# The rings of weight slabs move from the start of the SBUF partition to its end

## The chip, the cores and the metric

The kernel runs on one core of one Trainium2 chip. The metric is the device time of one execution in microseconds (us), as the median of several runs. Engines are named as the profile names them: PE is TensorE's matmuls and PEld its weight loads, DVE is VectorE, ACT is ScalarE, POOL is GpSimd, SP is the engine that issues nearly all DMA transfers.

## What is computed

Two blocks, one after the other, on 256 tokens of width 1,024, all in float32. The reference, cut to its frame:

```python
def first_block(x, ...):                      # DEPTH = 2 layers
    for l in range(DEPTH):
        h = rms_norm(x, norm_mix[l])
        proj = h @ w_in[l]                    # 1024 x 5120
        y_a = dilated_attention(dq, dk, dv) @ w_proj_a[l]
        y_b = stick_breaking_attention(sq, sk, sv) @ w_proj_b[l]
        gates = jax.nn.sigmoid(gate_logits + b_gate[l])
        x = x + (gates[..., :D_MODEL] * y_a + gates[..., D_MODEL:] * y_b) @ w_out[l]
        x = x + conv_ffn(rms_norm(x, norm_ffn[l]), w_up[l], conv_w[l], conv_b[l], w_down[l])
    return rms_norm(x, norm_final)

def hybrid_layer(x, ...):                     # second block, one layer
    proj = rmsnorm(x, norm_mix_w) @ w_in      # conv, gated delta rule, gated linear recurrence
    x = x + concat(gdn_out, lru_out) @ w_out
    u = relu(rmsnorm(x, norm_mlp_w) @ w_ff1)
    x = x + (u * u) @ w_ff2
```

## The kernel before

**Slabs.** Every large weight matrix is cut into slabs of at most 128 partitions by 2,048 float32 values (`SLAB`), mostly 256 output columns of the matrix in 8 chunks of 128 rows. `Plan` lists them once, in the order in which TensorE consumes them. A slab goes through three steps:

1. SP loads it from HBM into the ring `raw` (L648).
2. ACT writes its high part, rounded to the format `float32r`, into the ring `w_hi` (its copies all pass through one helper, so they show as L1329).
3. DVE (L1861) or, for a few slabs, POOL (L2614) writes the low part, `raw` minus `w_hi`, into the ring `w_lo`.

**Rings.** Each of the three rings has `SLOTS` = 3 slots of 2,048 values, that is 24,576 bytes in each partition. Slab n uses slot n modulo 3 of all three. SP loads slab n when the low part of slab n - 3 is written, since then nothing reads that slot of `raw` any more. ACT overwrites a slot of `w_hi` when the matmuls of slab n - 3 are done.

**Matmuls.** TensorE multiplies each chunk of a slab three times: high weight by high activation, high weight by low activation, low weight by high activation. The helper on L679 issues them. In most tiles the weights are the stationary operand and the activations (`xg_hi`, `xg_lo`, or the pairs in `hid_both`) the moving one of 256 columns; where a high part meets a `hid_both` pair, the high and low activations go through together as 512 columns. Only in the slabs of values and in the very last product are the weights the moving operand. The first slab alone is multiplied straight from `raw` in float32, by activations in `scratch`.

**The other tensors.** `xt` is the running x, `consts` and `params` are tables, `sq`, `rs`, `cs`, `rtok`, `gfg2` and `small` are small working tensors, and `scratch` (14,976 values) holds everything else: the token input, queries and keys, gates, attention probabilities `prob` and their transposes, the convolution rows, the output rows. Attention turns `prob` blocks on TensorE with the identity from `consts` (L906), and the last stage turns `xt` in the same way (L1259).

**Who is ordered by what.** Each engine's program is written out by hand in its order, with semaphores between engines. No order and no wait depends on where a tensor lies in the partition.

**Where a tensor lies.** The function `sb` asks for the tensors one after another, and the allocator puts each behind the one before, from byte 16,512 of the partition on (16,384 bytes and four small constants of the framework lie below), each start rounded up to a multiple of 32 bytes. The three rings are the first three requests; `scratch` is the last, and it ends at byte 225,632.

Of the kernel before, what the change touches and what calls it, by code (L numbers as in the profile page):

```python
# [25 lines left out]
F32R = mybir.dt.float32r  # L26
# [63 lines left out]
SLOTS = 3  # L90
RAWS = 1
IDLE_TURNS = 12
SLAB = 2048
# [305 lines left out]
def build(nc, w, consts_d, params_d, lru_d, out):  # L399
    plan = Plan(w)  # L400
    with ExitStack() as ctx:
        S = {n: ctx.enter_context(nc.semaphore(n)) for n in SEMS}

        def sb(name, cols, dt=F32):
            return ctx.enter_context(nc.sbuf_tensor("sb_" + name, [P, cols], dt))[:, :]

        raw = sb("raw", SLOTS * SLAB)
        w_hi = sb("w_hi", SLOTS * SLAB, F32R)
        w_lo = sb("w_lo", SLOTS * SLAB, F32R)
        xt = sb("xt", KD * T)  # L410
        xg_hi = sb("xg_hi", KD * T, F32R)
        xg_lo = sb("xg_lo", KD * T, F32R)
# [7 lines left out]
        gfg2 = sb("gfg2", KD)  # L420
        small = sb("small", 144)
        scratch = sb("scratch", SCRATCH)
        psum = ctx.enter_context(nc.psum_tensor("psum", [P, 8, 512], F32))

        def C(name, a=0, b=None):
# [2287 lines left out]
```

How the kernel before makes its waits and increments, by code:

```python
        @block.sync  # L623
# [13 lines left out]
                load_x(n)  # L637
            s = plan.slabs[0]
            for name, chunks in (("load_half", slice(0, KD // 2)), ("slab_in0", slice(KD // 2, KD))):
                eng.dma_start(by_chunk(raw, s)[:, chunks, :], s.src.rearrange("(k p) c -> p k c", p=P)[:, chunks, :])\
                    .then_inc(S[name], 16)
            for s in plan.slabs[1:]:
                if s.n >= SLOTS:
                    name, value = plan.slabs[s.n - SLOTS].low
                    if q.due(name, value):
                        eng.wait_ge(S[name], value)
                eng.dma_start(by_chunk(raw, s), s.src.rearrange("(k p) c -> p k c", p=P))\
                    .then_inc(S[f"slab_in{s.n % SLOTS}"], 16)
                if s.n == 2:
                    eng.dma_start(COS.bitcast(I32), w["positions"].to_broadcast([P, T])).then_inc(S["load_pos"], 16)
                    eng.dma_start(cst[:, EARLY:], consts_d[:, EARLY:]).then_inc(S["load_rest"], 16)
                if s.stage == (2, "in") and s.index == 3:
                    if q.due("q_tile", 12 * DEPTH):
                        eng.wait_ge(S["q_tile"], 12 * DEPTH)
                    eng.dma_start(l_w, lru_d).then_inc(S["load_lru"], 16)
                if s.stage == (2, "up", 0) and s.index == 3:
                    if q.due("x_tile", KD + 24 * DEPTH + 2 * KD):
                        eng.wait_ge(S["x_tile"], KD + 24 * DEPTH + 2 * KD)
                    if q.due("hid_lo", LO_BEFORE_MLP):
```

## Time and profile before

| | |
|---|---|
| median of 3 runs | 1070.47 us (1070.12 to 1070.49) |
| span of the profiled execution | 1068.9 us |
| PE busy | 1054.3 us (99%) |
| PEld busy | 1003.1 us (94%) |
| DVE busy | 720.5 us (67%) |
| ACT busy | 573.1 us (54%) |
| POOL busy | 284.9 us (27%) |
| mean DMA rate | 169 GB/s |

The span runs from the first to the last instruction of one profiled execution; the timed runs lie 1.6 us above it. Busy time of PE counts pipelined matmuls from issue to modelled end, so that two neighbours overlap: the pace of a stretch is read from the starts of its matmuls, and what sets the end of the program from the chain of work that ended last. A granted clock of 1.00 is TensorE at 2.4 GHz, 0.50 at 1.2 GHz.

### The profile page before, as it was taken

The numbers are of one execution on the slowest core, as the hardware profiler recorded it, in microseconds if no ns is written. First come the engines' busy times: TensorE is split into PE (matmuls) and PEld (weight loads), VectorE is DVE, ScalarE is ACT, GpSimd is POOL, SyncE is SP. The second block draws the span as 40 slices with busy tenths as digits, with TensorE's granted clock in tenths as the row PEclk, the third lists the DMA queues.
The fourth block names the chain that finished last, engine by engine and source line by source line (L and its number), as shares of the span: only waits on it lengthen the run. The fifth ranks groups of instructions, "written<-read, shape, count | busy, mean of one in ns | idle before, by whom it ended". The sixth has DMA issues, their size and how long they took to land.

```text
span 1068.9 us, 20016 instructions
## 1 busy us (share of the span) xinstructions
PE 1054.3 (99%) x8398; PEld 1003.1 (94%) x8398; DVE 720.5 (67%) x1217; ACT 573.1 (54%) x791; POOL 284.9 (27%) x179
## 2 busy tenths in 40 slices
PE   8999999999999999999999999999899999999997
PEld 7999998999999899999999989998899999999996
DVE  5762248887677775322878857777887789666763
ACT  6454466654354644545765534556557865343443
POOL 0376665100000137666640000013300034101020
PEclk9999999999999999999999999999999999999999
DMA  9644444465653664444456566446333157563751
GB/s 308 202 161 140 156 159 158 163 212 157 222 193 124 214 215 158 131 148 150 157 165 213 160 217 200 132 147 217 110 94 116 60 178 224 186 209 126 249 170 40
DMA packets 169705, 180.11 MB, mean 169 GB/s; under 512 B 4240, under 2 KB 166416, under 8 KB 169488
## 3 DMA queue, kind: packets, MB, share of 16 engines
q1 hardware_dynamic: 169616, 178.84, 52.3%
q8 instruction: 66, 1.08, 0.4%
q14 instruction: 23, 0.19, 0.1%
HBM read 177.78 MB, written 1.05 MB: 167 GB/s over the span
## 4 chain that ended last, share of the span: by engine, by line
PE 88%; DVE 4%; ACT 3%; POOL 2%; issue 1%; DMA 1%; SPq 0%; POOLq 0%; ACTq 0%; DVEq 0%
PE psum L679 87%; DVE sb_w_lo L1861 2%; POOL sb_w_lo L2614 1%; ACT sb_scratch L1329 1%; ACT sb_w_hi L1329 1%; DVE sb_xg_lo L1845 1%; POOL sb_scratch L2654 1%; DMA sb_raw<-in_w_in 1%; PE psum L906 1%; DVE psum L1845 1%; DVE sb_scratch L1845 0%; ACT L1329 0%; DVE sb_hid_both L1936 0%; DVE sb_xt L1879 0%; DVE sb_scratch L2439 0%
## 5 line engine op out<-in xcount | busy, mean ns | idle before, releaser
L1329 ACT ACTIVATE sb_w_hi<-sb_raw 128x2048 fp32r<-128x2048 f32 (+3 forms) x185 | 318.2, 1724 | 175.4 <-PE psum L679 111.1
L679 PE MATMUL psum<-sb_xg_hi,sb_w_hi 128*128 128x256 f32 x1656 | 411.9, 287 | 0.0
L679 PE MATMUL psum<-sb_xg_lo,sb_w_hi 128*128 128x256 f32 x1656 | 406.6, 284 | 0.0
L1861 DVE TENSOR_TENSOR sb_w_lo<-sb_raw,sb_w_hi 128x2048 fp32r<-128x2048 f32 (+3 forms) x150 | 305.6, 2040 | 110.7 <-ACT sb_w_hi L1329 109.9
L679 PEld LDWEIGHTS psum<-sb_xg_hi,sb_w_hi 128*128 128x128 f32 x1656 | 317.3, 192 | 3.2 <-DVE sb_xg_lo L1845 0.7
L679 PEld LDWEIGHTS psum<-sb_xg_lo,sb_w_hi 128*128 128x128 f32 x1656 | 317.9, 192 | 0.3
L679 PE MATMUL psum<-sb_xg_hi,sb_w_lo 128*128 128x256 f32 x1656 | 233.7, 284 | 0.1
L679 PEld LDWEIGHTS psum<-sb_xg_hi,sb_w_lo 128*128 128x128 f32 x1656 | 213.6, 192 | 0.9 <-DVE sb_w_lo L1861 0.3
L679 PE MATMUL psum<-sb_hid_both,sb_w_hi 128*128 128x512 f32 (+1 forms) x912 | 210.0, 364 | 0.4 <-DVE sb_xt L1879 0.2
L2614 POOL TENSOR_TENSOR sb_w_lo<-sb_raw,sb_w_hi 128x2048 fp32r<-128x2048 f32 (+1 forms) x34 | 156.1, 4598 | 110.3 <-ACT sb_w_hi L1329 100.8
L679 PEld LDWEIGHTS psum<-sb_hid_both,sb_w_hi 128*128 128x128 f32 x912 | 150.4, 190 | 20.8 <-issue 0.8
L679 PEld LDWEIGHTS psum<-sb_hid_both,sb_w_lo 128*128 128x128 f32 x784 | 112.5, 190 | 9.4
L679 PE MATMUL psum<-sb_hid_both,sb_w_lo 128*128 128x256 f32 x784 | 119.7, 283 | 0.0
L2630 POOL TENSOR_TENSOR sb_rs<-sb_sq 128x256 f32<-128x256 f32 x6 | 4.8, 804 | 325.4 <-ACT sb_sq L1329 325.4
L1329 ACT ACTIVATE sb_hid_both<-sb_scratch 128x256 fp32r<-128x256 f32 x100 | 38.5, 414 | 98.3 <-DVE sb_scratch L2151 68.8
L2686 POOL TENSOR_TENSOR sb_scratch<-sb_scratch 128x256 f32<-128x256 f32 x32 | 23.3, 751 | 123.2 <-DVE sb_scratch L1845 123.2
L1329 ACT ACTIVATE sb_scratch<-sb_scratch,sb_params 128x256 f32<-128x256 f32 x76 | 37.8, 554 | 31.3 <-DVE sb_scratch L2148 31.3
L1936 DVE TENSOR_TENSOR sb_hid_both<-sb_scratch,sb_hid_both 128x256 fp32r<-128x256 f32 x100 | 50.7, 545 | 4.8 <-ACT sb_hid_both L1329 4.3
L679 PE MATMUL psum<-sb_scratch 64*64 64x32 f32 (+6 forms) x728 | 49.7, 263 | 3.0 <-ACT sb_scratch L1329 3.0
L2020 DVE CUSTOM_DVE_ANT_0 sb_scratch<-psum,sb_consts 128x512 f32<-128x512 f32 x16 | 10.4, 689 | 61.9 <-PE psum L679 61.9
L679 PEld LDWEIGHTS psum<-sb_scratch 64*64 64x64 f32 (+3 forms) x728 | 42.0, 152 | 8.9 <-ACT sb_scratch L1329 3.2
L1329 ACT ACTIVATE sb_scratch<-psum 128x256 f32<-128x256 f32 (+3 forms) x58 | 24.6, 463 | 47.7 <-PE psum L679 28.6
(172 smaller groups left out, 986.1 us busy)
## 6 DMA issues: line engine op xcount, KB each, us to landing
sb_raw<-in_w_in SPq DMA_DIRECT2D x51, 1024.0 KB, 5.2
sb_raw<-in_w_up SPq DMA_DIRECT2D x44, 1024.0 KB, 5.1
sb_raw<-in_w_ff SPq DMA_DIRECT2D x21, 1024.0 KB, 5.7
sb_raw<-in_w_down SPq DMA_DIRECT2D x16, 768.0 KB, 4.7
sb_raw<-in_w_down SPq DMA_DIRECT2D x16, 640.0 KB, 4.4
sb_raw<-in_w_out SPq DMA_DIRECT2D x8, 1024.0 KB, 5.1
sb_raw<-in_w_ff SPq DMA_DIRECT2D x8, 768.0 KB, 4.6
sb_raw<-in_w_ff SPq DMA_DIRECT2D x8, 640.0 KB, 4.5
```

The lines of the kernel that those rows point to most:

```text
L679: return nc.tensor.matmul(ps, lhsT, rhs, start=start, stop=stop, skip_group_check=True)
L906: mm = nc.tensor.transpose(psum[:, BANK_T + u % 2, i * P:i * P + P], prob_of(u)[:, i * P:i * P + P], C("ident"))
L1329: return nc.scalar.activation(out_, in_, func, **kw)
L1845: return v.scalar_tensor_tensor(out=out_, in0=a, scalar=scalar, in1=b, op0=op0, op1=op1)
L1861: v.tensor_tensor(part(w_lo, s), part(raw, s), part(w_hi, s).bitcast(F32), ALU.subtract)\
L1936: v.tensor_tensor(hid_lo(i), src, hid_hi(i).bitcast(F32), ALU.subtract).then_inc(S["hid_lo"], 1)
L2020: v.tensor_tensor_reduce(prob_of(u), psum[:, BANK_SC + u % 2, :], C(f"dil_mask{units(u)[1]}"), -HEAD ** -0.5, 3e38, ALU.add, ALU.min, dil_ ...
L2614: g.tensor_tensor(part(w_lo, s), part(raw, s), part(w_hi, s).bitcast(F32), ALU.subtract)\
L2630: g.tensor_tensor(SUMS[n], tl(sq, 2 * n) if m == 1 else SUMS[n], tl(sq, 2 * n + m % 2), ALU.add)\
L2654: g.tensor_tensor(tl(mix32, m % 4), tl(mixA, m % 2), tl(mixB, m % 4), ALU.add)\
L2686: g.tensor_tensor(tl(h32, i % 4), tl(y_conv, i % 4), tl(y_conv, i % 4), ALU.mult)\
```

## The change

The three lines that allocate `raw`, `w_hi` and `w_lo` move from the head of the list of tensors to its end, behind `scratch`. Nothing else differs.

```diff
-        raw = sb("raw", SLOTS * SLAB)
-        w_hi = sb("w_hi", SLOTS * SLAB, F32R)
-        w_lo = sb("w_lo", SLOTS * SLAB, F32R)
         xt = sb("xt", KD * T)
         xg_hi = sb("xg_hi", KD * T, F32R)
...
         small = sb("small", 144)
         scratch = sb("scratch", SCRATCH)
+        raw = sb("raw", SLOTS * SLAB)
+        w_hi = sb("w_hi", SLOTS * SLAB, F32R)
+        w_lo = sb("w_lo", SLOTS * SLAB, F32R)
         psum = ctx.enter_context(nc.psum_tensor("psum", [P, 8, 512], F32))
```

The order of instructions on PE, DVE, ACT, POOL and SP is the same in both programs, row for row, with the same operands, shapes and waits. What differs is the start address, in bytes from the start of each partition:

| tensor | bytes | start before | start after | remainder by 64, before and after |
|---|---|---|---|---|
| `raw` | 24,576 | 16,512 | 151,904 | 0, 32 |
| `w_hi` | 24,576 | 41,088 | 176,480 | 0, 32 |
| `w_lo` | 24,576 | 65,664 | 201,056 | 0, 32 |
| `xt` | 8,192 | 90,240 | 16,512 | 0, 0 |
| `xg_hi` | 8,192 | 98,432 | 24,704 | 0, 0 |
| `xg_lo` | 8,192 | 106,624 | 32,896 | 0, 0 |
| `hid_both` | 24,576 | 114,816 | 41,088 | 0, 0 |
| `consts` | 9,920 | 139,392 | 65,664 | 0, 0 |
| `cs` | 4,096 | 160,992 | 87,264 | 32, 32 |
| `scratch` | 59,904 | 165,728 | 92,000 | 32, 32 |

Every tensor that isn't a ring comes down by 73,728 bytes, which is 36 times 2,048. The rings go up by 135,392 bytes, which is 66 times 2,048 and 224 over; their distances from each other stay. Before, `prob`, part of `scratch`, starts at byte 206,688; after, `w_lo` covers bytes 201,056 to 225,632.

## Rows read from the trace of the kernel before

**Rows 1.** The chain that ended last: shares by line, and its first piece (start, us)
```profile
PE psum L679 87%; DVE sb_w_lo L1861 2%; POOL sb_w_lo L2614 1%; ACT sb_scratch L1329 1%; ACT sb_w_hi L1329 1%; DVE sb_xg_lo L1845 1%; POOL sb_scratch L2654 1%; DMA sb_raw<-in_w_in 1%; PE psum L906 1%; DVE psum L1845 1%; DVE sb_scratch L1845 0%; ACT L1329 0%; DVE sb_hid_both L1936 0%; DVE sb_xt L1879 0%; DVE sb_scratch L2439 0%
...
3.63 6.53 DMA sb_raw<-in_w_in
```

**Rows 2.** Two stretches: length, busy us of PE, PEld, DVE, ACT, POOL, clock, DMA share, GB/s
```profile
142.00:175.00 33.00, 32.84 (x240) 30.49 (x239) 22.79 (x40) 22.91 (x39) 23.14 (x14) 1.00 0.51 162
...
733.00:854.00 121.00, 117.57 (x1314) 110.46 (x1311) 95.44 (x209) 81.69 (x143) 18.25 (x8) 0.99 0.35 109
```

**Rows 3.** Costliest groups of the page: moving then stationary operand, xcount | busy, mean ns
```profile
L679 PE MATMUL psum<-sb_xg_hi,sb_w_hi 128*128 128x256 f32 x1656 | 411.9, 287 | 0.0
L679 PE MATMUL psum<-sb_xg_lo,sb_w_hi 128*128 128x256 f32 x1656 | 406.6, 284 | 0.0
...
L679 PE MATMUL psum<-sb_xg_hi,sb_w_lo 128*128 128x256 f32 x1656 | 233.7, 284 | 0.1
...
L679 PE MATMUL psum<-sb_hid_both,sb_w_hi 128*128 128x512 f32 (+1 forms) x912 | 210.0, 364 | 0.4 <-DVE sb_xt L1879 0.2
...
L679 PE MATMUL psum<-sb_hid_both,sb_w_lo 128*128 128x256 f32 x784 | 119.7, 283 | 0.0
```

**Rows 4.** Timeline of PE at 95 us: start, us, instruction
```profile
95.43 0.28 PE L679 MATMUL psum<-sb_xg_lo,sb_w_hi 128*128 128x256 f32 x1
95.55 1.12 PE L679 MATMUL psum<-sb_xg_hi,sb_w_lo 128*128 128x256 f32 x8
```

**Rows 5.** Instructions of L906, L1259, sb_raw, sb_cs: xcount: ns min/median/max, first and last start
```profile
L906 PE MATMUL psum<-sb_consts,sb_scratch x64: 270/273/273, 96.5 to 501.6; 128*128 128x128 f32 x64
...
L906 PEld LDWEIGHTS psum<-sb_consts,sb_scratch x64: 138/141/144, 96.4 to 501.5; 128*128 128x128 f32 x64
...
L1259 PEld LDWEIGHTS psum<-sb_consts,sb_xt x16: 139/140/143, 1019.3 to 1021.0; 128*128 128x128 f32 x16
L1259 PE MATMUL psum<-sb_consts,sb_xt x16: 271/273/273, 1019.5 to 1021.1; 128*128 128x128 f32 x16
...
L679 PEld LDWEIGHTS psum<-sb_scratch,sb_raw x32: 187/190/191, 10.2 to 16.8; 128*128 128x128 f32 x32
...
L679 PEld LDWEIGHTS psum<-sb_scratch,sb_cs x16: 187/191/192, 803.0 to 821.7; 128*128 128x128 f32 x16
```

**Rows 6.** Groups of DVE, ACT and POOL, shapes kept apart, 1,024 values per partition
```profile
L1861 DVE TENSOR_TENSOR sb_w_lo<-sb_raw,sb_w_hi 128x1024 fp32r<-128x1024 f32 x6 | 7.3, 1218 | 1.7 <-ACT sb_w_hi L1329 1.7
...
L2417 DVE TENSOR_TENSOR sb_scratch<-sb_scratch 128x1024 f32<-128x1024 f32 x1 | 1.2, 1226 | 0.0
L1329 ACT ACTIVATE sb_w_hi<-sb_raw 128x1024 fp32r<-128x1024 f32 x8 | 8.3, 1048 | 2.5 <-PE psum L679 2.5
...
L1329 ACT ACTIVATE sb_scratch<-sb_scratch 128x1024 f32<-128x1024 f32 x3 | 3.2, 1055 | 0.5 <-DVE sb_scratch L2417 0.5
L2614 POOL TENSOR_TENSOR sb_w_lo<-sb_raw,sb_w_hi 128x1024 fp32r<-128x1024 f32 x2 | 4.7, 2392 | 32.2 <-ACT sb_w_hi L1329 32.2
...
L2677 POOL TENSOR_TENSOR sb_sq<-sb_sq,sb_scratch 128x1024 f32<-128x1024 f32 x1 | 2.4, 2362 | 51.1 <-ACT sb_sq L1329 51.1
```

**Rows 7.** DMA: hardware queue of the page, SP's longest wait, two windows (last two: share, GB/s)
```profile
q1 hardware_dynamic: 169616, 178.84, 52.3%
...
SPq L648 <- DVE sb_w_lo L1861: 731.0, 147, 14.5
...
12.00:13.00 1.00, 1.00 (x6) 0.87 (x6) 1.00 (x4) 1.00 (x5) 0.00 (x0) 1.00 1.11 349
...
889.00:890.00 1.00, 1.00 (x11) 1.00 (x10) 1.00 (x1) 0.00 (x0) 1.00 (x1) 1.00 1.04 366
```

**Rows 8.** Three windows around 760 us, columns as in rows 2 (the clock is third from last)
```profile
758.00:760.00 2.00, 0.57 (x5) 0.57 (x6) 1.31 (x4) 1.28 (x3) 0.00 (x0) 1.00 1.01 352
760.00:762.00 2.00, 2.00 (x15) 2.00 (x14) 0.93 (x8) 2.00 (x3) 0.00 (x0) 0.65 0.41 137
762.00:764.00 2.00, 2.00 (x11) 2.00 (x10) 1.65 (x12) 1.95 (x2) 0.00 (x0) 0.50 0.00 0
```

## The prediction

> **What bounds the kernel now.** I read the chain of work that ended last first, because it says which engine's time is the program's time: the helper through which TensorE's matmuls are issued holds 87% of it [rows 1]. The rest, some 13% or 139 us of the profiled 1068.9 us, is spread over DVE, ACT, POOL and DMA. Then come the stretches: in the two where TensorE hands over most often, its busy time is still 32.84 of 33.00 us and 117.57 of 121.00 us [rows 2]. So the kernel goes at the pace of its matmuls. Third, the costliest groups: 1656 + 1656 + 1656 + 912 + 784 = 6,664 matmuls take their stationary operand from `w_hi` or `w_lo`, which are two of the three tensors that change their place [rows 3]. Fourth, their pace from the timeline: one starts at 95.43 us and the next at 95.55, 0.12 us later, and the eight behind it fill 1.12 us, which is seven steps of 0.12 us and one duration of 0.28 [rows 4]. The question of this case is therefore narrow: does TensorE's 0.12 us step, or any duration beside it, depend on the address of an operand?
>
> **The change, part by part.** No instruction is added, removed or reordered, no wait and no semaphore differs, and no transfer changes its size, so there is no queue past which anything moves. What can change is the duration of work that touches a moved address. Three properties of an address differ: the rings' remainder by 64 bytes (0 before, 32 after), their position (all three then lie where `scratch` lay before, `w_lo` under its tail), and their distance to the activations. The other tensors keep their remainder by 2,048 and only come down; I cost them at nothing, since their neighbours in the rows below show no dependence on position either.
>
> (a) Weight loads and matmuls. The trace has the same operation on both kinds of address. The transposes of L906 take `prob` as their stationary operand, at byte 206,688 and above with a remainder of 32 by 64: just the kind of address the rings get. Those of L1259 take `xt`, at byte 90,240, remainder 0: the kind that the rings leave. Their weight loads have a median of 141 and 140 ns, their matmuls of 273 and 273 ns [rows 5]. A second pair is of the weight loads ahead of float32 matmuls of 256 columns: 190 ns with `raw` as stationary operand (remainder 0), 191 ns with `cs` (remainder 32) [rows 5]. The two ends for a ring matmul are thus 0 and +1 ns. For 6,664 of them +1 ns would be 6.7 us. I take 0, because the PE matmul of the closest pair, L906 against L1259, does not differ at all and the weight load, which differs by 1 ns in the median, lies beside the matmul before it, and because ranges within each group (138 to 144, 139 to 143) are wider than the difference. Below nothing: a stationary load of ring data would have to gain from the new place; neither pair shows the higher or odd address as the cheaper one. Term: 0 us.
>
> Distance to the activations: before, a matmul of `xg_hi` with `w_hi` joins tensors 57,344 bytes apart, and one with `w_lo` 32,768 bytes apart. Both step by 0.12 us [rows 4], 287 and 284 ns mean [rows 3]. A pace that hung on the distance would show two values here. Term: 0 us.
>
> (b) Splits. The copies into `w_hi` and the subtractions into `w_lo` touch only ring tensors, whose distances stay. With 1,024 values per partition, DVE takes 1218 ns on ring addresses and 1226 on `scratch` (remainder 32); ACT 1048 against 1055; POOL 2392 against 2362 [rows 6]. So the bounds are +0.7% for DVE and ACT, and -1.3% for POOL. On the chain they have 2% (DVE L1861), 1% (ACT) and 1% (POOL L2614) [rows 1], some 21, 11 and 11 us. The term lies between 21 x 0.7% + 11 x 0.7% = +0.2 us and 11 x -1.3% = -0.1 us. The rows compare an operation of one kind with one of another, so this small difference need not be of the address; I take 0.
>
> (c) Transfers into `raw`. They keep their size and number and arrive at a start with remainder 32. The hardware queue is busy for 52.3% of the span, and SP stands 731.0 us in 147 waits for a slot that DVE frees [rows 7]: a somewhat longer transfer is taken from that wait, and ends at no engine. Only the first load is exposed, 6.53 us of the chain [rows 1]. A comparison: between 12 and 13 us, with slabs going to ring addresses, the DMA moves 349 GB/s at a share of 1.11, that is 314 per full share; between 889 and 890 us, when the output gain is being spread into `scratch` (remainder 32) beside slabs, 366 at 1.04, that is 352 [rows 7]. The second has larger pieces, so it is no clean measure, but it excludes that a start with remainder 32 is costly. Bounds: 314 / 352 is -11% of 6.53 us, -0.7 us; the mirror of it above is +0.7 us. I take 0.
>
> The rows point to no dependence at all. The Trainium skill has one rule that would: "DMA: Bandwidth & Descriptors", section "How a descriptor splits into AXI transactions", says that a transfer not starting at a multiple of 256 bytes first goes down to the boundary below and pays for the bytes in between. It speaks of what is fetched; if it held for the SBUF side of these loads too, a piece of 1,024 bytes would be an estimated 36 beats before (remainder 128 by 256) and 35 after (remainder 96), the exposed load would be 3% or 0.2 us shorter, and the sum -0.2 us in place of 0. No row here shows single beats.
>
> (d) The clock. At 760 to 764 us the granted clock is 0.65 and then 0.50, behind a window in which TensorE was busy for only 0.57 of 2 us; the lost time is 2 x 0.35 + 2 x 0.50 = 1.7 us [rows 8]. It is at the level of 1.2 GHz for that stretch. If a small shift in time let it come otherwise, the sum could move by 1.7 us either way, still under 0.2%. I take 0.
>
> Sum: 0 us against the profiled span of 1068.9 us, which with the 1.6 us outside the span gives the median as it was: 1070.5 us.
>
> **The rivals.** About 0.2%, 2.1 us, is what a measurement of this kernel can tell from no change.
>
> Slower, by the matmuls: operands with a remainder of 32 by 64, or at the end of the partition, cost TensorE's read a step. For it speaks only that weight loads of `cs` and `prob` have a median 1 ns above their partners; against it that the matmuls of L906 and L1259 are equal [rows 5]. At +1 ns for each of 6,664 matmuls the time is 1070.5 + 6.7 = 1077.2 us; if only the 1656 + 784 = 2,440 with `w_lo` pay, 1072.9 us. It decides from 2.1 us / 6,664 = 0.3 ns each. Chance 5%.
>
> Slower, by the transfers: writes to the new addresses take longer by a factor f. The first load alone makes 0.2% at f = 1.33 (6.53 x 0.33 = 2.1 us). Later it decides where DMA becomes the bound, at f = 1 / 0.523 = 1.9; with f = 2 the queue would be busy 1068.9 x 0.523 x 2 = 1118 us, and the time about 1120 us. Against it is the window at 889 us [rows 7]. Chance 2%.
>
> Faster: the old neighbourhood of rings and activations costs TensorE something that the new one doesn't. No row names what makes up the step of 0.12 us, so it could hold such a cost; against it is that the step is the same for both distances [rows 4]. 1 ns less each gives 1070.5 - 6.7 = 1063.8 us. Chance 3%.
>
> The change does not do what it says: the allocator could sort its requests, and the addresses would stay. It doesn't, since the built program has the new starts; and the time would be 1070.5 us all the same. Inside the forecast.
>
> Clock and chance: two or more stretches at the lower clock come or go, at 1.7 us each, 1067 or 1074 us. 1% each way.
>
> **How the numbers follow.** The forecast, no change, has 88%. Faster by over 0.2% is 3% + 1% = 4%; slower is 5% + 2% + 1% = 8%; within 0.2% is 88%. The range takes in the bounds that were left open: splits -0.1 and +0.2, the first load -0.7 and +0.7, the clock -1.7 and +1.7, together -2.5 and +2.6 us, so 1068.0 to 1073.1 us. That also holds the rival in which only `w_lo` pays, and leaves out under 1 in 10.
>
> **What would show it.** Right: the slab matmuls still step by 0.12 us with means of 284 and 287 ns, LDWEIGHTS of the rings have the same mean, the 2,048-value splits of the three engines keep theirs, the first DMA piece of the chain is near 6.5 us, and the chain is at TensorE's helper for 87%. Wrong: a step of 0.121 us or more (or below 0.119), or ring weight loads longer than those of other operands, tells of TensorE; longer splits in the two stretches of handovers, without a change in the step, tell of the engines; more "DMA" among the releasers of ACT's copies tells of the transfers. What would make the prediction wrong as a whole is a property of the partition that no tensor of the kernel before exposes, such as one that shows only when the moving operand, the stationary operand and a write are all at particular places at once.

## The result and the profile after

The changed kernel takes 1056.22 us (median of 4 runs, 1055.63 to 1059.37), the kernel before 1070.48 us beside it: a ratio of 0.986, 95% interval 0.9844 to 0.9877. The forecast was no change, 1070.5 us, range 1068.0 to 1073.1. It was wrong: a change of addresses alone gained 1.4%. The profiled execution has a span of 1053.9 us, 15.0 us under the one before.

The page after, from its groups (operands as in [rows 3]; xcount | busy, mean ns | idle before):

```profile
L679 PE MATMUL psum<-sb_xg_hi,sb_w_hi 128*128 128x256 f32 x1656 | 401.8, 283 | 0.1
L679 PE MATMUL psum<-sb_xg_lo,sb_w_hi 128*128 128x256 f32 x1656 | 396.7, 279 | 0.0
...
L679 PE MATMUL psum<-sb_xg_hi,sb_w_lo 128*128 128x256 f32 x1656 | 228.3, 280 | 0.1
L679 PE MATMUL psum<-sb_hid_both,sb_w_hi 128*128 128x512 f32 (+1 forms) x912 | 210.5, 364 | 1.3 <-DVE sb_xt L1874 0.6
...
L679 PE MATMUL psum<-sb_hid_both,sb_w_lo 128*128 128x256 f32 x784 | 118.2, 279 | 0.0
```

Against [rows 3], every group of 256 columns is 3 to 5 ns shorter (287 to 283, 284 to 279, 284 to 280, 283 to 279), and the group that is mostly of 512 columns is not (364 and 364). The timeline of PE shows the pace (start, us, instruction):

```profile
93.24 0.28 PE L679 MATMUL psum<-sb_xg_lo,sb_w_hi 128*128 128x256 f32 x1
93.35 0.28 PE L679 MATMUL psum<-sb_xg_hi,sb_w_hi 128*128 128x256 f32 x1
93.47 0.28 PE L679 MATMUL psum<-sb_xg_lo,sb_w_hi 128*128 128x256 f32 x1
93.59 0.28 PE L679 MATMUL psum<-sb_xg_hi,sb_w_hi 128*128 128x256 f32 x1
93.70 0.28 PE L679 MATMUL psum<-sb_xg_lo,sb_w_hi 128*128 128x256 f32 x1
...
94.52 1.10 PE L679 MATMUL psum<-sb_xg_hi,sb_w_lo 128*128 128x256 f32 x8
```

Four steps take 93.70 - 93.24 = 0.46 us, where each took 0.12 before [rows 4]. A finer measure is used from here on: in a stage of even tiles, the starts of two neighbouring groups of eight matmuls with `w_lo` are one tile of 24 matmuls apart. Starts are shown to 0.01 us, so such a step is good to 0.4 ns. The first two lines are of the kernel before, the last two of the one after:

```profile
208.08 1.12 PE L679 MATMUL psum<-sb_xg_hi,sb_w_lo 128*128 128x256 f32 x8
210.96 1.12 PE L679 MATMUL psum<-sb_xg_hi,sb_w_lo 128*128 128x256 f32 x8
```

```profile
208.26 1.10 PE L679 MATMUL psum<-sb_xg_hi,sb_w_lo 128*128 128x256 f32 x8
211.06 1.10 PE L679 MATMUL psum<-sb_xg_hi,sb_w_lo 128*128 128x256 f32 x8
```

2.88 us / 24 = 120.0 ns before, 2.80 us / 24 = 116.7 ns after. That is under the 0.119 us which the prediction named as the sign that TensorE's work had changed. The weight loads of the rings that stand beside these matmuls are shorter too, with a mean of 188 ns against 192. The other engines' work is nearly what it was: DVE is busy for 720.2 us (720.5 before), ACT 572.9 (573.1), POOL 287.1 (284.9), and the hardware DMA queue for 53.0% of the span against [rows 7]'s 52.3%.

**Where the 15 us come from.** I summed the distances between the starts of all matmuls of both traces. 5,899 steps of the slab matmuls of 256 columns with a stationary ring operand (gaps above 130 ns left out) take 706.5 us before and 689.3 after: -17.2. Gaps behind slab matmuls grow from 31.2 to 33.6 us: +2.4. The last stage, 512 columns with the ring as the moving operand, goes from 27.0 to 27.8 us: +0.8. The rest is -1.0, and it is the clock's: before, the granted clock is 0.50 for 3.4 us from 760.6 us on [rows 8], and in the profile after there is no such drop at that place. TensorE starts 26 matmuls between 760 and 764 us before, and 40 in the four microseconds after that do the same work (749 to 753, clock 1.00). Step by step, the matmuls under the drop are 1.6 us slower than the same ones after: 1.0 us of it in the rest, 0.6 in the gaps. So some 1.6 of the 15.0 us are not the step's, but an event that differs from one execution to the next; the kernel `a2_front_shifted` below has the same step, keeps the drop (at 749.5 us), and has a span of 1054.9 us. The grown gaps stand where TensorE now reaches the other engines. The chain, cut to the end of the second half of `w_down` in layer 0, before and then after (shares by line of that stretch):

```profile
by line: PE psum L679 100.7%
...
343.83 30.22 PE psum L679 x179
```

```profile
by line: PE psum L679 31.4%; DVE sb_w_lo L1861 24.2%; ACT sb_w_hi L1329 15.2%; DVE sb_xt L1879 9.1%; DVE sb_xt L1877 7.3%; ACT sb_xg_hi L1329 5.3%; issue 4.5%; DVE sb_xg_lo L1845 4.2%; ACT sb_sq L1329 0.3%; ACTq L1342 0.1%
...
348.67 1.29 ACT sb_w_hi L1329
349.98 1.49 DVE sb_w_lo L1861
```

Before, that stretch was TensorE's alone. With a shorter step, much of what ends last in it is work of DVE and ACT, the splits of the slabs above all.

### The profile page after: what moved, and what is told of

Same layout as the page of the kernel before. It is cut to its first block, busy times and chain, and to the rows that moved or that the text cites. A ratio compares the mean times of both kernels' runs of the same rounds, so it can differ in the third digit from the quotient of the medians.

```text
span 1053.9 us, 20016 instructions
## 1 busy us (share of the span) xinstructions
PE 1039.0 (99%) x8398; PEld 984.3 (93%) x8398; DVE 720.2 (68%) x1217; ACT 572.9 (54%) x791; POOL 287.1 (27%) x179
## 4 chain that ended last, share of the span: by engine, by line
PE 84%; DVE 7%; ACT 4%; POOL 2%; issue 2%; DMA 1%; SPq 0%; POOLq 0%; ACTq 0%; DVEq 0%
PE psum L679 83%; DVE sb_w_lo L1861 2%; POOL sb_w_lo L2614 1%; ACT sb_scratch L1329 1%; ACT sb_w_hi L1329 1%; DVE sb_xg_lo L1845 1%; DVE psum L1845 1%; POOL sb_scratch L2654 1%; DMA sb_raw<-in_w_ff 1%; DMA sb_raw<-in_w_in 1%; PE psum L906 1%; DVE sb_hid_both L1936 0%; DVE sb_xt L1879 0%; DVE sb_scratch L1845 0%; DVE sb_xt L1877 0%
## 5 line engine op out<-in xcount | busy, mean ns | idle before, releaser
L679 PE MATMUL psum<-sb_xg_hi,sb_w_hi 128*128 128x256 f32 x1656 | 401.8, 283 | 0.1
L679 PE MATMUL psum<-sb_xg_lo,sb_w_hi 128*128 128x256 f32 x1656 | 396.7, 279 | 0.0
L679 PEld LDWEIGHTS psum<-sb_xg_hi,sb_w_hi 128*128 128x128 f32 x1656 | 310.3, 187 | 3.3 <-DVE sb_xg_lo L1845 0.8
L679 PEld LDWEIGHTS psum<-sb_xg_lo,sb_w_hi 128*128 128x128 f32 x1656 | 310.7, 188 | 0.3
L679 PE MATMUL psum<-sb_xg_hi,sb_w_lo 128*128 128x256 f32 x1656 | 228.3, 280 | 0.1
L679 PEld LDWEIGHTS psum<-sb_xg_hi,sb_w_lo 128*128 128x128 f32 x1656 | 207.9, 187 | 1.0 <-DVE sb_w_lo L1861 0.3
```

What stands on the lines that cost most here:

```text
L679: return nc.tensor.matmul(ps, lhsT, rhs, start=start, stop=stop, skip_group_check=True)
```

## Experiments

Three theories stood against each other. **C**: the step depends on where a matmul's stationary operand lies relative to its moving one. **S**: it depends on the remainder by 64 of the stationary operand's own address. **P**: it depends on the position in the partition, or on the distance in tens of KB. "Relation" below is the start of the stationary tensor less that of the moving one, by 256 bytes. It is 0 for every matmul with `w_hi` or `w_lo` as stationary operand before (all starts have remainder 128 by 2,048) and 224 after (352 less 128). A step from one chunk to the next moves both operands by 1,024 bytes, the other half of a slab the stationary one by 512, another slot by 8,192, so that the relation is the same in a whole kernel.

**Rings at the end, relation 0.**

```diff
         scratch = sb("scratch", SCRATCH)
+        sb("gap", 456)
+        raw = sb("raw", SLOTS * SLAB)
```

> Rings at the end as in the changed kernel, but 1,824 bytes further, so that each ring's start has the remainder by 2,048 that it had before (128), the same as the activations. Theory C (what sets the step of a slab matmul is where its stationary operand lies relative to the moving one, by a power of two of at most 2,048 bytes): step back to 0.120 us, time 1070.5 us. Theory S (remainder by 64 of the stationary operand alone): the same, 1070.5 us. Theory P (position in the partition, or distance to the activations in tens of KB): step 0.117 us, 1056 us.

Measured: 1071.67 us (10 runs), ratio 1.0011 (0.9999 to 1.0023). Its groups:

```profile
L680 PE MATMUL psum<-sb_xg_hi,sb_w_hi 128*128 128x256 f32 x1648 | 409.7, 286 | 0.0
L680 PE MATMUL psum<-sb_xg_lo,sb_w_hi 128*128 128x256 f32 x1648 | 404.4, 283 | 0.0
L680 PE MATMUL psum<-sb_xg_hi,sb_w_lo 128*128 128x256 f32 x1648 | 232.2, 284 | 0.1
```

All as before. The end of the partition gives nothing: P falls.

**Rings at the front, relation 224.**

```diff
+        sb("gap", 56)
         raw = sb("raw", SLOTS * SLAB)
         w_hi = sb("w_hi", SLOTS * SLAB, F32R)
         w_lo = sb("w_lo", SLOTS * SLAB, F32R)
+        sb("gap2", 456)
         xt = sb("xt", KD * T)
```

> Rings at the front as before, but 224 bytes further, and all other tensors 2,048 bytes further, so that rings and activations stand to each other by 2,048 as in the changed kernel (352 against 128). Theory C: step 0.117 us, 1056 us. Theory S: the same. Theory P: 0.120 us, 1070.5 us.

Measured: 1056.1 us (4 runs), ratio 0.9866 (0.9847 to 0.9885), the same as the changed kernel's. Means of the three groups: 283, 279 and 280 ns, as after. The whole gain is had at the old place, with 224 bytes.

**Everything 32 bytes further.**

```diff
+        sb("gap", 8)
         raw = sb("raw", SLOTS * SLAB)
```

> The kernel before with every tensor 32 bytes further: the rings' remainder by 64 becomes 32, as in the changed kernel, and so does the activations'; their relation stays. Theory C: step 0.120 us, 1070.5 us. Theory S: step 0.117 us, 1056 us. Theory P: 1070.5 us.

Measured: 1071.02 us (10 runs), ratio 1.0007 (0.9998 to 1.0017). The rings have remainder 32 by 64 here, as in the changed kernel, and nothing is gained: S falls. Of the three, C is left.

**A map of relations.** Next, each slot of `w_hi` and `w_lo` got an offset of its own, so that one kernel shows three relations (here 32, 64 and 96; the other tensors stand 2,048 bytes further):

```diff
-        w_hi = sb("w_hi", SLOTS * SLAB, F32R)
-        w_lo = sb("w_lo", SLOTS * SLAB, F32R)
+        w_hi = sb("w_hi", SLOTS * SLAB + 256, F32R)
+        w_lo = sb("w_lo", SLOTS * SLAB + 256, F32R)
...
-            return buf[:, i * SLAB:i * SLAB + s.chunks * s.cols]
+            at = i * SLAB + ((8, 16, 24)[i] if buf is w_hi else (8, 16, 24)[i] if buf is w_lo else 0)
+            return buf[:, at:at + s.chunks * s.cols]
```

The first of them had six relations: the lists were (8, 16, 32) for `w_hi` and (0, 24, 48) for `w_lo`, in columns of four bytes:

> Rings at the front; every slot of w_hi and w_lo has an offset of its own against the activations, by 256 bytes: w_hi +32, +64, +128, w_lo 0 (+256), +96, +192. Theory C: six steps, seen slot by slot; +224 gave 0.1167 us and 0 gave 0.120; if the relation counts by 256 or less, slot 0 of w_lo has 0.120 us, and some slot may be faster than 0.1167. Theory S: +32, +96 at 0.117 us and +64, +128, +192, +256 at 0.120 us. Theory P: all 0.120 us.

Measured: 1062.57 us (one run). Its parts of tiles (16 matmuls with `w_hi`, 8 with `w_lo`) have mean steps between 113.6 and 120.6 ns. But in a tile `w_hi` and `w_lo` stand in different relations, and slot 1, with `w_hi` at 64, has 117.9 ns in one half of a slab and 113.6 in the other. One reading is that a part takes on the rhythm of the part ahead of it; no run tests it by itself. For a map this was the wrong design, and the next five give both rings the same offset: (8, 16, 24) columns as above, then (32, 40, 48), (64, 80, 96), (12, 20, 112) and (4, 52, 60).

> Rings at the front, the other tensors 2,048 bytes further; in w_hi and w_lo alike slot 0 lies 32, slot 1 64 and slot 2 96 bytes further against the activations. Theory C (the relation of stationary and moving operand sets the step): steady tiles show a step of their own for each slot and for each half of a slab (the halves stand 512 bytes apart). From the kernel of six offsets: slot 1 has about 0.1133 us in one half and 0.118 in the other; slots 0 and 2 lie between 0.1167 and 0.120. If only an exact coincidence (0 and 512) costs, all six are 0.1167 or below and the time is 1056 us or less. Theory S: slots 0 and 2 at 0.1167, slot 1 at 0.120 us.

> The same with 128, 160 and 192 bytes. Theory C, smooth in the offset: steps fall on from 96 to 192 towards or below the 0.1167 us of 224; Theory C with a period of 64 or 128 bytes: slot 0 as at 0, 0.120 us, slot 2 as at 64.

> The same with 256, 320 and 384 bytes. Theory C with a period of 256 bytes: slot 0 at 0.120 us, slot 1 as slot 1 at 64, slot 2 as at 128. With the full period of 512 or 1,024: three new values, 320 mirroring 192 if only the distance to the nearest coincidence counts.

> Slots of w_hi and w_lo at 48, 80 and 448 bytes against the activations. Theory C, with cells of 32 bytes or less: 48 and 80 differ from 64. If the relation is symmetric about 512, slot 2 (448 = 512 - 64) steps by 0.1133 us like 64; if it has a sign, by a value of its own. 48 bytes: between 0.1133 and 0.1183 us if smooth.

> Slots of w_hi and w_lo at 16, 208 and 240 bytes against the activations. If the relation acts in units of 16 bytes, 16 differs from both 0 (0.120) and 32 (0.1183 us); 240 may be the mirror of 16 and 208 of 48. If in units of 32, 16 is equal to 0 or to 32.

Measured: 1058.39, 1065.85, 1064.57, 1064.33 and 1061.46 us (one run each; the kernel before took 1070.8 to 1072.7 beside them). The rows of the kernel with 32, 64 and 96, its slots 0, 1 and 2 in turn, two tiles each:

```profile
190.25 1.11 PE L680 MATMUL psum<-sb_xg_hi,sb_w_lo 128*128 128x256 f32 x8
193.09 1.11 PE L680 MATMUL psum<-sb_xg_hi,sb_w_lo 128*128 128x256 f32 x8
195.84 1.07 PE L680 MATMUL psum<-sb_xg_hi,sb_w_lo 128*128 128x256 f32 x8
198.56 1.07 PE L680 MATMUL psum<-sb_xg_hi,sb_w_lo 128*128 128x256 f32 x8
201.40 1.12 PE L680 MATMUL psum<-sb_xg_hi,sb_w_lo 128*128 128x256 f32 x8
204.28 1.12 PE L680 MATMUL psum<-sb_xg_hi,sb_w_lo 128*128 128x256 f32 x8
```

Slot 0: 2.84 us / 24 = 118.3 ns. Slot 1: 2.72 / 24 = 113.3. Slot 2: 2.88 / 24 = 120.0. In the same way, from the same stage of each kernel:

| offset of slot, bytes | 0 | 16 | 32 | 48 | 64 | 80 | 96 | 128 | 160 | 192 | 208 | 224 | 240 | 256 | 320 | 384 | 448 |
|---|---|---|---|---|---|---|---|---|---|---|---|---|---|---|---|---|---|
| step, ns | 120.0 | 118.3 | 118.3 | 118.3 | 113.3 | 118.8 | 120.0 | 118.8 | 120.0 | 117.9 | 116.7 | 116.7 | 120.0 | 120.0 | 117.5 | 118.8 | 117.9 |

Each value rests on one tile, and neighbours such as 117.5 and 117.9, or 118.3 and 118.8, are one or two units of the last digit apart. I therefore took all tiles of each trace that lie within one slab and have no gap in them, some 30 per offset, at full nanoseconds. Nine offsets keep to one step: 0, 160 and 256 to 120.0, 32 to 118.3, 208 and 224 to 116.7, 80, 128 and 384 to 118.5 to 119.0 (one tile of 128 and one of 224 apart). The others have several steps in one and the same execution:

| offset of slot, bytes | 16 | 48 | 64 | 96 | 192 | 240 | 320 | 448 |
|---|---|---|---|---|---|---|---|---|
| step, ns (tiles) | 118.3 (26), 120.0 (2) | 117.8 (20), 118.3 (7) | 113.3 (25), 117.8 (4) | 120.0 (20), 118.5 (5), 117.3 (5) | 117.8 (29), 113.3 (1) | 120.0 (16), 117.2 to 117.5 (14) | 117.8 (24), 113.3 (5) | 117.8 (29), 113.3 (1) |

One of the tiles at 240 that isn't at 120.0 (2.82 / 24 = 117.5):

```profile
569.49 1.10 PE L680 MATMUL psum<-sb_xg_hi,sb_w_lo 128*128 128x256 f32 x8
572.31 1.10 PE L680 MATMUL psum<-sb_xg_hi,sb_w_lo 128*128 128x256 f32 x8
```

So the step is not smooth in the offset, remainder 32 by 64 is neither good nor bad (32, 96, 160, 224: 118.3, 120.0, 120.0, 116.7), and no offset keeps a step above that of 0. The pairs 0 and 256, 128 and 384, 192 and 448 agree; 64 and 320 have the same two steps, in other shares. My guess that only the distance from a coincidence counts is wrong: 32 has 118.3 and 224, its mirror, 116.7.

**The best relation, everywhere.**

```diff
         w_lo = sb("w_lo", SLOTS * SLAB, F32R)
+        sb("gap", 496)
         xt = sb("xt", KD * T)
```

> The rings stay where the kernel before has them; every other tensor lies 1,984 bytes further, so that each ring starts 64 bytes past the activations by 2,048 (128 against 64). Theory C: the step of 0.1133 us that slot 1 had at 64 holds for all slots, whichever of the two tensors was moved: the 6,008 matmuls of 256 columns with a stationary ring operand save 6.7 ns each, 40 us, of which the changed kernel's ratio (14 us measured of 3.3 ns x 6,008 = 20 us) lets 29 us through: about 1041 us, between 1031 and 1048. Theory S (rings' own remainder, here as before): 1070.5 us.

Measured: 1051.02 us (4 runs, 1045.87 to 1052.77), ratio 0.9803 (0.9774 to 0.9832). The rings have not moved against the kernel before, only the others have, and the step goes to 113.3 ns, the same as when only the rings moved by 64 (slot 1 above). The address of one operand alone doesn't explain that, and with both moved by 32 bytes nothing changed (`a3_all_plus32`): it is the relation. But the time is 10 us above what was expected, so I ran it a second time on another chip, and built a kernel that splits the effect by tensor.

> The kernel c1_all_64 once more, to see whether its rhythm belongs to the program or to the execution. If to the program: steps of 0.1133 us in the same tiles, 1051 us with a spread like 3 us. If a stretch can fall into either of the two rhythms that the two kernels with 64 bytes showed (0.1133 and 0.1178 us) from one execution to the next: tiles at 0.1178 in other places, and times between 1045 and 1054 us.

The kernel that splits it has `hid_both` moved back into relation 0:

```diff
         w_lo = sb("w_lo", SLOTS * SLAB, F32R)
+        sb("gap", 496)
         xt = sb("xt", KD * T)
         xg_hi = sb("xg_hi", KD * T, F32R)
         xg_lo = sb("xg_lo", KD * T, F32R)
+        sb("gap2", 16)
         hid_both = sb("hid_both", 2 * HID * T, F32R)
```

> As the kernel c1_all_64, but hid_both lies 64 bytes further, so that it has the relation to the rings that it had before (128 and 128), and only xt, xg_hi and xg_lo have the 64. Theory C, tensor by tensor: matmuls with xg step by 0.1133 us, those with hid_both by 0.120 us (256 columns) and 0.231 us (512 columns), the last stage by 0.2267 us as before. 4,968 matmuls save 6.7 ns, 33 us, of which 24 us come through: about 1046 us. It is faster than c1 only if 64 costs the 512-column matmuls more than it saves for the 1,040 others with hid_both.

Measured: 1049.96 us (1049.26 to 1050.2), ratio 0.9799 (0.9779 to 0.9819), and for the second 1053.68 us, ratio 0.9827 (0.9807 to 0.9847). First the kernel `c1_all_64` in two stages, then the same program in its second profile:

```profile
207.26 1.07 PE L680 MATMUL psum<-sb_xg_hi,sb_w_lo 128*128 128x256 f32 x8
209.98 1.07 PE L680 MATMUL psum<-sb_xg_hi,sb_w_lo 128*128 128x256 f32 x8
...
289.50 1.07 PE L680 MATMUL psum<-sb_xg_hi,sb_w_lo 128*128 128x256 f32 x8
292.22 1.07 PE L680 MATMUL psum<-sb_xg_hi,sb_w_lo 128*128 128x256 f32 x8
```

```profile
206.79 1.10 PE L680 MATMUL psum<-sb_xg_hi,sb_w_lo 128*128 128x256 f32 x8
209.62 1.10 PE L680 MATMUL psum<-sb_xg_hi,sb_w_lo 128*128 128x256 f32 x8
...
287.95 1.07 PE L680 MATMUL psum<-sb_xg_hi,sb_w_lo 128*128 128x256 f32 x8
290.68 1.07 PE L680 MATMUL psum<-sb_xg_hi,sb_w_lo 128*128 128x256 f32 x8
```

The same program steps by 113.3 ns (2.72 / 24) in both stages of one execution, and by 117.9 (2.83 / 24) in the first stage of another. The second execution has the other rhythm just ahead of that, and changes at a gap of about half a microsecond (3.29 us from one group to the next, in place of 2.72):

```profile
200.78 1.07 PE L680 MATMUL psum<-sb_xg_hi,sb_w_lo 128*128 128x256 f32 x8
203.50 1.07 PE L680 MATMUL psum<-sb_xg_hi,sb_w_lo 128*128 128x256 f32 x8
206.79 1.10 PE L680 MATMUL psum<-sb_xg_hi,sb_w_lo 128*128 128x256 f32 x8
```

It goes the other way round as well: in the first tiles with `w_ff1` the step is 117.9 ns in `c1_all_64` (866.25 to 869.08 us, 2.83 / 24) and 113.3 in the second execution (871.60 to 874.32). So at 64 there are two rhythms, and a stretch keeps the one that it falls into until a gap in the stream. Both rhythms stand in both profiles: over all tiles, 117.8 ns has 17 of 87 in the first and 30 of 87 in the second.

The kernel that gives only `xg` the 64 bytes keeps, for matmuls with `hid_both`, what the kernel before has, while those with `xg` are faster (three groups of it: one with `xg_lo`, two with `hid_both`):

```profile
L681 PE MATMUL psum<-sb_xg_lo,sb_w_hi 128*128 128x256 f32 x1648 | 389.7, 278 | 0.0
...
L681 PE MATMUL psum<-sb_hid_both,sb_w_lo 128*128 128x256 f32 x784 | 120.0, 283 | 0.0
...
L681 PE MATMUL psum<-sb_w_hi,sb_hid_both 128*128 128x512 f32 x80 | 24.7, 389 | 0.0
```

So it is the relation of the rings to the tensor that is streamed with them, not to some third tensor. Whether what counts is a matmul's own two operands, or its moving operand and the weights that are loaded beside it for the next one, these kernels don't tell apart: within a part of a tile both stand in the same relation.

**Only `xg_lo`.**

```diff
+        sb("gap", 496)
         xg_lo = sb("xg_lo", KD * T, F32R)
+        sb("gap2", 16)
         hid_both = sb("hid_both", 2 * HID * T, F32R)
```

> As the kernel before, but xg_lo lies so that the rings are 64 bytes past it by 2,048; xg_hi, hid_both and everything else keep their relation. Theory C, taken at the moving operand of each matmul: tiles of w_lo, which stream xg_hi alone, keep 0.120 us; in tiles of w_hi, where xg_hi and xg_lo take turns, the step lies between 0.1133 and 0.120 us. About 1060 us. If instead the relation between rings and some other tensor, or of any two writes, made the difference: no change, 1070.5 us.

Measured: 1062.29 us (one run). Half is as expected: `hid_both` with `w_lo` has 283 ns as before, and tiles of `xg` take 2.82 / 24 = 117.5 ns. Half is not: the `w_lo` part of a tile, which streams `xg_hi` in relation 0, does not come to 120 but stays near 118 ns. It may be that eight matmuls are too few to leave the rhythm of the sixteen ahead of them; that is not shown.

**64 + 256.**

```diff
         w_lo = sb("w_lo", SLOTS * SLAB, F32R)
+        sb("gap", 432)
         xt = sb("xt", KD * T)
```

> As c1_all_64 with 320 bytes (64 + 256) between rings and activations. If the relation counts by 256 bytes (0 and 256, 128 and 384, 192 and 448 had equal steps): the rhythms of 64, 0.1133 or 0.1178 us, and 1045 to 1054 us. If it counts by 512: 0.1178 us throughout, as slot 1 had at 320, and about 1060 us.

Measured: 1047.25 us (4 runs, 1044.43 to 1047.99), ratio 0.9771 (0.9749 to 0.9792), the fastest kernel of the study, 9 us under the changed one. That 320 is better than 64 is not shown: the ranges of `c1_all_64` and this kernel overlap, and both have both rhythms. Its two stages:

```profile
205.82 1.10 PE L680 MATMUL psum<-sb_xg_hi,sb_w_lo 128*128 128x256 f32 x8
208.65 1.10 PE L680 MATMUL psum<-sb_xg_hi,sb_w_lo 128*128 128x256 f32 x8
...
289.70 1.07 PE L680 MATMUL psum<-sb_xg_hi,sb_w_lo 128*128 128x256 f32 x8
292.43 1.07 PE L680 MATMUL psum<-sb_xg_hi,sb_w_lo 128*128 128x256 f32 x8
```

2.83 and 2.73 us per tile: both rhythms of 64, at 320. All four pairs 256 bytes apart agree, and the relation counts by 256 bytes.

**Why it stops there.** With the step at 113.3 ns, 6.7 ns for 6,008 matmuls would be 40 us. `c1_all_64` gained 24.8 us of span (1068.9 to 1044.1). By the sum over starts, its slab matmuls of 256 columns take 674.3 us against 706.5, -32.2 and not -40, since part of them run at 117.8 ns, and the gaps grow by 6.7 us. Its chain shows the same:

```profile
by line: PE psum L680 73.8%; DVE sb_w_lo L1862 3.4%; ACT sb_w_hi L1330 2.9%; issue 2.5%; ACT sb_scratch L1330 2.0%; POOL sb_w_lo L2615 1.4%; POOL sb_scratch L2646 1.3%; DMA sb_raw<-in_w_in 1.3%; DVE sb_xg_lo L1846 0.9%; DVE psum L1846 0.8%;
```

TensorE's helper has 73.8% of it, where it had 87% [rows 1]. What a shorter step brings from here is shared with the splits.

## Why the prediction was wrong

**What bounds the kernel: right.** TensorE's step was the program's time, and the question "does 0.12 us depend on an address" was the right one. The gain, 17.2 us before losses, is in that step, but for the 1.6 us of the clock.

**Step (a), weight loads and matmuls: wrong, and this is the step that failed.** I put the slab matmuls' term at 0; it measured -17.2 us, 3.3 ns for each step of an even stage. I took 0 from two comparisons in [rows 5]. Both pairs are float32 matmuls, which have another pace, and where their relation differs they don't show it. L906 stands in relation 224 (206,688 less 139,392 is 224 by 256), before and after, since `prob` and `consts` move together; L1259 stands in 0. So the first pair compared just the two relations of this change, and both have 273 ns. The product straight from `raw`, whose relation went from 32 to 0, has a mean of 382 ns after 383. The slab matmuls are of the format `float32r`, and no float32 matmul stands in for them. I noted that the comparison was of the address, not that it was of another kind of matmul. I also compared durations, not steps. And I excluded a gain ("below nothing") because neither of two float32 pairs showed one, which was no reason.

**Distance to the activations: wrong.** "A pace that hung on the distance would show two values" at 57,344 and 32,768 bytes. It would, if those two distances differed in what counts. Both are multiples of 256, as is every distance between rings and activations in that layout: the trace held one relation, 0, in 6,664 instances, and the one with the longest step. The row could not tell.

**Steps (b) and (c): right; (d) within its bound.** The splits kept their durations (DVE's have a median of 2,284 ns in both), and the queue its busy share to 0.7 points. The clock has a mean of 0.998 in both profiles, but the low stretch at 760 us that (d) priced at 1.7 us did not come, as said above; it explains a tenth of the difference. The splits are paid for in another way: they end last in stretches that were TensorE's, +2.4 us in the gaps (3.0 with the clock's 0.6 taken out), which no step of mine had.

**The rival "faster, by the old neighbourhood"** named the mechanism, and I gave it 3%. Its price was mis-sized: 1 ns each gave 1063.8 us, while the term measured 3.3 ns on the 256-column steps. Nor was it the neighbourhood in the sense of place: `a2_front_shifted` has the whole gain at the old one. Against it I set only the two distances. The reason for it, that no row tells what makes up the step, deserved more: a term of zero for 1,000 us of bound time rests on the trace having shown both cases, and it had shown one.

**The page's rule.** What the Trainium skill says in "DMA: Bandwidth & Descriptors" on starts that are no multiple of 256 bytes is about transfers. It shows no part in the result: the one exposed load, which by the estimate from it would be 0.2 us shorter, has 6.53 us on the chain before and after. The 256 bytes of this case are a matter of TensorE's two operands.

**What stays open.** Shown is that the step of a `float32r` matmul of 256 columns depends on the relation of its two operands by 256 bytes, and that a stretch can have two rhythms. Not shown is why. The reading that the weight load of the next matmul and the moving operand of the present one meet in the same part of SBUF fits that only their relation counts, and that a rhythm, once there, stays; but no run took the load away from beside the stream. Why 64 and 320 often step by 113.3 ns, where 192 and 448 do so in one tile each and the rest of the map never, is open too; the map has one execution of each offset. The effect is shown with the ring as the stationary operand. The 384 matmuls of 256 columns in which the ring is the moving one take 47.2 us before, 47.1 after and 47.0 in `c1_all_64` by the sum over starts.

## What to carry to other kernels

Where TensorE's step bounds a kernel of many equal matmuls, the starts of the stationary and the moving tensor, by 256 bytes, are a parameter to sweep: unused bytes between two allocations gave 2.3% here. Tensors laid one behind the other whose sizes are multiples of 256 bytes stand in relation 0 by default, and none of the relations tried was slower. A trace can only exclude a dependence if it has shown two values of what may matter, in the same kind of instruction. Judge such a change by steps between starts in an even stage, since one execution may keep another rhythm than the next.

## What the runs showed of the hardware

- The step of `float32r` matmuls, 128 x 128 stationary and 256 columns moving, is 120.0 ns at relation 0 and between 113.3 and 120.0 at others, at a granted clock of 1.00. Neither the place in the partition (rings at the end, 1071.67 us) nor 32 bytes more for every tensor (1071.02 us) changed it, and 64 bytes give 113.3 ns whichever of the two operands is moved.
- At 512 columns relation 0 is not the slow one: the last stage of the program, with the ring as moving operand, has a mean duration of 390 ns at relation 0, 395 to 396 after the change, and 393 (`w_hi`) and 388 (`w_lo`) in `c1_all_64`.
- Float32 matmuls showed no difference: 273 ns for transposes of 128 columns at 224 and 0, 383 and 382 ns for 256 columns at 32 and 0.
- In a relation of 64 the same stage runs at 113.3 ns in one execution and 117.9 in another, and the switch comes at a gap in the stream. The relation 240 has tiles of 117.5 and of 120.0 ns in one execution.
